# Stick-breaking layer: scores and values as three rounded matmuls instead of one fp32 matmul, with both halves of a later weight split moved behind the gated products

## What is computed

```python
z = jnp.einsum('bqhd,bshd->bhqs', qblk, kk)                      # scores
sp = jnp.where(visible, jax.nn.softplus(z), 0.0)
tw = jnp.einsum('bhqks,sj->bhqkj', sp, upper)                    # sums over later keys
w = jnp.exp(jnp.where(visible, z - tail, -jnp.inf))
return jnp.einsum('bhqs,bshd->bqhd', w, vv)                      # values
...
q, k, v, gate = jnp.split(h @ w_in, [B_WIDTH, 2 * B_WIDTH, 3 * B_WIDTH], axis=-1)
return (o * jax.nn.silu(gate)) @ w_out
```

## Time and profile before

| what | value |
|---|---|
| median of 3 runs (lowest, highest) | 903.99 us (903.72, 904.41) |
| time of the profiled execution | 904.42 us |
| its span, first to last instruction | 902.7 us |
| TensorE busy | 893.0 us, 99% |
| VectorE busy | 551.5 us, 61% |
| ScalarE busy | 430.4 us, 48% |
| chain that ended last | TensorE 96% |

### The profile page before, as it was taken

How to read it: one execution, slowest core, us unless ns; L and a number is a source line. 1 busy time by engine, 2 the same in 40 slices (tenths; PEclk the granted TensorE clock), 3 DMA queues, 4 the chain that set the end, 5 groups by cost and what they waited for, 6 DMA issues and landing times.

```text
span 902.7 us, 17891 instructions
## 1 busy us (share of the span) xinstructions
PE 893.0 (99%) x7182; PEld 861.6 (95%) x7182; DVE 551.5 (61%) x752; ACT 430.4 (48%) x685; POOL 56.4 (6%) x85
## 2 busy tenths in 40 slices
PE   9999999999999999999999999999999999999997
PEld 9999999999999999899999999999999999988886
DVE  6577667666755767785646464555646355545546
ACT  6556455645555344385454443535444444435421
POOL 1322112312200000000000000000000000000000
PEclk9999999999999999999999999999999999999999
DMA  9676465546442555425353434444453534454622
GB/s 351 232 236 180 154 209 134 156 160 190 131 155 114 187 187 191 183 69 211 142 187 139 180 145 169 156 147 178 139 186 139 186 144 165 156 218 156 233 93 94
DMA packets 25256, 153.06 MB, mean 170 GB/s; under 512 B 3410, under 2 KB 3938, under 8 KB 8708
## 3 DMA queue, kind: packets, MB, share of 16 engines
q1 hardware_dynamic: 21600, 142.19, 43.1%
q0 software_dynamic: 2896, 7.70, 4.5%
q10 hardware_dynamic: 724, 2.66, 0.8%
HBM read 150.36 MB, written 2.18 MB: 169 GB/s over the span
## 4 chain that ended last, share of the span: by engine, by line
PE 96%; DMA 1%; DVE 1%; SPq 1%; ACT 0%; issue 0%; DVEq 0%
PE bank L336 72%; PE bank L716 10%; PE bank L495 2%; PE bank L453 2%; DMA work<-chunks 1%; PE bank L661 1%; PE bank L660 1%; PE bank L663 1%; PE bank L628 1%; PE bank L587 1%; PE bank L601 1%; PE bank L470 1%; PE bank L629 0%; PE bank L588 0%; PE bank L471 0%; PE bank L702 0%
## 5 line engine op out<-in xcount | busy, mean ns | idle before, releaser
L336 PE MATMUL bank<-x_hi,w_hi 128*128 128x272 f32 (+1 forms) x1472 | 425.1, 289 | 0.0
L336 PE MATMUL bank<-x_hi,w_lo 128*128 128x272 f32 (+1 forms) x1472 | 421.5, 286 | 0.0
L336 PE MATMUL bank<-x_lo,w_hi 128*128 128x272 f32 (+1 forms) x1472 | 421.4, 286 | 0.0
L1078 DVE TENSOR_TENSOR w_lo<-raw,w_hi 128x2048 fp32r<-128x2048 f32 x126 | 291.0, 2313 | 209.8 <-ACT w_hi L795 177.3
L795 ACT ACTIVATE w_hi<-raw 128x2048 fp32r<-128x2048 f32 x114 | 218.0, 1913 | 156.9 <-PE bank L336 104.5
L336 PEld LDWEIGHTS bank<-x_hi,w_hi 128*128 128x128 f32 x1472 | 277.4, 188 | 0.9 <-issue 0.2
L336 PEld LDWEIGHTS bank<-x_hi,w_lo 128*128 128x128 f32 x1472 | 277.4, 188 | 0.0
L336 PEld LDWEIGHTS bank<-x_lo,w_hi 128*128 128x128 f32 x1472 | 277.1, 188 | 0.0
L336 PE MATMUL bank<-og_hi,w_hi 128*128 128x272 f32 x240 | 70.1, 292 | 0.0
L336 PE MATMUL bank<-og_hi,w_lo 128*128 128x272 f32 x240 | 69.4, 289 | 0.0
L336 PE MATMUL bank<-og_lo,w_hi 128*128 128x272 f32 x240 | 69.1, 288 | 0.0
(11 more groups left out here) (247 smaller groups left out, 1008.4 us busy)
## 6 DMA issues: line engine op xcount, KB each, us to landing
raw<-chunks SPq DMA_DIRECT2D x128, 1024.0 KB, 4.8
work<-bias_table POOLq DMA_DIRECT2D x8, 512.0 KB, 5.7
work<-chunks SPq DMA_DIRECT2D x4, 512.0 KB, 12.6
work<-bias_table POOLq DMA_DIRECT2D x8, 256.0 KB, 6.9
work<-ln_rows ACTq DMA_DIRECT2D x1, 2048.0 KB, 6.9
out<-work SPq DMA_DIRECT2D x8, 256.0 KB, 2.4
h<-xT SPq DMA_DIRECT2D x2, 544.0 KB, 9.2
raw<-chunks SPq DMA_DIRECT2D x4, 256.0 KB, 4.9
```

The source lines that it names most:

```text
L336: last = mm(o, l, r, start=(kt == 0 and n == 0), stop=(kt == KT - 1 and n == 2))
L1078: V.tensor_tensor(lo_part, raw[:, half, :, :], hi_part.bitcast(f32), ALU.subtract) \
```

## The change

Scores and values are made like the projections, from hi and lo parts. For the scores ScalarE makes rounded queries (`qb_parts[0]`) and keys (`kb_parts[0]`) and VectorE the rests; for the values ScalarE makes a rounded copy of the weights w and takes the turned values out of PSUM as rounded, and VectorE makes the rests. The parts lie in buffers that are free at that time (`parts_r`, the last two tiles of `og_hi` and `og_lo`) and two new tiles. Every matmul of `scores_b` and `attend_b` becomes three in fp32r. VectorE's `split_lo(P+5, 0)` and `split_lo(P+5, 1)` both go to the end of the body, behind the gated products. Besides, `neg_ones_r` shrinks to one column that is read 128 times, and a spare identity goes; the spinning matmuls of the layer's start use `neg_upper_r` in its place.

```diff
@@ -89,10 +89,12 @@
...
-        ident_r = sb("ident_r", [128, 128], f32r)
+        last_hi = sb("last_hi", [128, 128], f32r)
+        last_lo = sb("last_lo", [128, 128], f32r)
...
-        neg_ones_r = sb("neg_ones_r", [128, 128], f32r)
+        neg_ones_r = sb("neg_ones_r", [128, 1], f32r)
+        neg_ones = neg_ones_r[:].to_broadcast([128, 128])
@@ -137,8 +139,12 @@
...
-        b = carve([("q", (2, SEQ)), ("kT", (2 * T,)), ("vT", (2 * T,)), ("V", (2, 256)), ("V_last", (128,)),
-                   ("w", (B_Z2,)), ("sp", (B_Z2,)), ("gate", (2, SEQ)), ("og", (SEQ,))])
+        b = carve([("q", (2, SEQ)), ("kT", (2 * T,)), ("vT", (2 * T,)), ("w", (B_Z2,)), ("sp", (B_Z2,)), ("gate", (2, SEQ)), ("og", (SEQ,))])
+        ends = [og.rearrange("p a b -> p (a b)")[:, (KT - 2) * T:KT * T] for og in (og_hi, og_lo)]
+        qb_parts = [flat_r[:, n * 2 * SEQ:(n + 1) * 2 * SEQ].rearrange("p (a b) -> p a b", b=SEQ) for n in range(2)]
+        kb_parts = [flat_r[:, 4 * SEQ:4 * SEQ + 2 * T], ends[1]]
+        vb_parts = [end[:, 0:512].rearrange("p (a b) -> p a b", b=256) for end in ends]
+        vb_last = (last_hi[:], last_lo[:])
@@ -579,17 +587,23 @@
...
             def scores_b(i):

-                for u in range(2):
-                    pe.wait_ge(tile_free[u], P_B + 4 * i + 2)
-                    z, q, k = z_bank[u], b["q"][:, u, :], b["kT"][:, B_KEYS[u]]
-                    if u == 0:
-                        pe.wait_ge(pt_copied, PT_A + 2 * i)
-                    mm(z[:, 0:B_K1], k[:, 0:128], q, start=True, stop=False)
-                    m = mm(z[:, B_K1:B_K2], k[:, 128:256], q[:, B_Q1:SEQ], start=False, stop=(u == 0))
+                pe.wait_ge(qb_lo, i + 1)
+                pe.wait_ge(kb_lo, i + 1)
+                pe.wait_ge(pt_copied, PT_A + 2 * i)
+                terms = [(kb_parts[m], qb_parts[n]) for m, n in ((0, 0), (0, 1), (1, 0))]
+                for u in range(2):
+                    z = z_bank[u]
+                    for n, (k, q) in enumerate(terms):
+                        mm(z[:, 0:B_K1], k[:, B_KEYS[u]][:, 0:128], q[:, u, :], start=(n == 0), stop=False)
+                    for n, (k, q) in enumerate(terms):
+                        m = mm(z[:, B_K1:B_K2], k[:, B_KEYS[u]][:, 128:256], q[:, u, B_Q1:SEQ], start=False,
+                               stop=(u == 0 and n == 2))
                     if u == 0:
                         m.then_inc(z_ready, 1)
                 z = z_bank[1][:, B_K2:B_K2 + B_L]
-                mm(z, b["kT"][:, B_ENDS], b["q"][:, :, B_Q2:SEQ], start=False, stop=True).then_inc(z_ready, 1)
+                for n, (k, q) in enumerate(terms):
+                    m = mm(z, k[:, B_ENDS], q[:, :, B_Q2:SEQ], start=False, stop=(n == 2))
+                m.then_inc(z_ready, 1)
@@ -621,14 +635,20 @@
...
             def attend_b(i):
-                pe.wait_ge(pt_copied, PT_A + 2 * (i + 1))
-                pe.wait_ge(vb_copied, 2 * (i + 1))
-                for u in range(2):
-                    o, w, v = o_b[:, u, :], b["w"][:, B_HEADS[u]], b["V"][:, u, :]
-                    mm(o, v[:, 0:128], w[:, 0:B_K1], start=(u == 0), stop=False)
-                    mm(o[:, B_Q1:SEQ], v[:, 128:256], w[:, B_K1:B_K2], start=False, stop=False)
-                last = b["w"][:, B_LAST].rearrange("p (a c) -> p a c", c=META)
-                mm(o_b[:, :, B_Q2:SEQ], b["V_last"], last, start=False, stop=True).then_inc(pv_done, 2)
+                pe.wait_ge(wb_lo, 2 * (i + 1))
+                pe.wait_ge(vb_lo, 2 * (i + 1))
+                terms = ((0, sp_hi), (1, sp_hi), (0, sp_lo))
+                for u in range(2):
+                    o = o_b[:, u, :]
+                    for n, (m, w) in enumerate(terms):
+                        mm(o, vb_parts[m][:, u, 0:128], w[:, B_HEADS[u]][:, 0:B_K1], start=(u == 0 and n == 0), stop=False)
+                    for m, w in terms:
+                        mm(o[:, B_Q1:SEQ], vb_parts[m][:, u, 128:256], w[:, B_HEADS[u]][:, B_K1:B_K2], start=False,
+                           stop=False)
+                for n, (m, w) in enumerate(terms):
+                    last = mm(o_b[:, :, B_Q2:SEQ], vb_last[m], w[:, B_LAST].rearrange("p (a c) -> p a c", c=META),
+                              start=False, stop=(n == 2))
+                last.then_inc(pv_done, 2)
@@ -990,6 +1009,9 @@
                     split_hi(P + 2, 0, True)
                 for u in range(2):
                     evac(P, u, b["q"][:, u, :], slice(0, SEQ), B_SCALE)
+                for u in range(2):
+                    act.wait_ge(tile_free[u], P + 1)
+                A(qb_parts[0], b["q"], ACT.Copy).then_inc(qb_hi, 1)
                 if not isinstance(i, int):
                     split_hi(P + 2, 1, True)
                     split_hi(P + 3, 0, True)
@@ -999,6 +1021,9 @@
...
                     A(b["kT"][:, B_KEYS[u]] if u else b["kT"][:, 0:T], k_acc[u][:, 0:SEQ if u else T], ACT.Copy) \
                         .then_inc(tile_free[u], 1)
+                for u in range(2):
+                    act.wait_ge(tile_free[u], P + 2)
+                A(kb_parts[0], b["kT"], ACT.Copy).then_inc(kb_hi, 1)
                 if isinstance(i, int):
                     split_hi(P + 3, 0, True)
                 split_hi(P + 3, 1, True)
@@ -1025,10 +1050,12 @@
                 for n, (z, w) in enumerate(parts):
                     act.wait_ge(tail_ready, 2 * i + n + 1)
                     A(w, z, ACT.Exp).then_inc(pt_copied, 1)
+                    act.wait_ge(pt_copied, PT_A + 2 * i + n + 1)
+                    A(sp_hi[:, B_HEADS[n]], w, ACT.Copy).then_inc(wb_hi, 1)
                 act.wait_ge(vtb_ready, 2 * i + 1)
-                A(b["V"].rearrange("p a b -> p (a b)"), v_turned[:], ACT.Copy).then_inc(vb_copied, 1)
+                A(vb_parts[0].rearrange("p a b -> p (a b)"), v_turned[:], ACT.Copy).then_inc(vb_copied, 1)
                 act.wait_ge(vtb_ready, 2 * i + 2)
-                A(b["V_last"], bank[5][:, 0:128], ACT.Copy).then_inc(vb_copied, 1)
+                A(vb_last[0], bank[5][:, 0:128], ACT.Copy).then_inc(vb_copied, 1)
@@ -1357,9 +1384,18 @@
             def body_b(i):
                 P = P_B + 4 * i

+                def queries_rest():
+                    dve.wait_ge(qb_hi, i + 1)
+                    V.tensor_tensor(qb_parts[1], b["q"], qb_parts[0].bitcast(f32), ALU.subtract).then_inc(qb_lo, 1)
+
                 if not isinstance(i, int):
+                    queries_rest()
                     split_lo(P + 2, 0, True)
                 split_lo(P + 2, 1, True)
+                if isinstance(i, int):
+                    queries_rest()
+                dve.wait_ge(kb_hi, i + 1)
+                V.tensor_tensor(kb_parts[1], b["kT"], kb_parts[0].bitcast(f32), ALU.subtract).then_inc(kb_lo, 1)
                 split_lo(P + 3, 0, True)
                 split_lo(P + 3, 1, True)
@@ -1390,7 +1426,15 @@
                     if u == 0 and isinstance(i, int):
                         split_lo(P + 4, 0, True)
                 split_lo(P + 4, 1, True)
-                split_lo(P + 5, 0, True)
+                for n, (z, w, s) in enumerate(parts):
+                    dve.wait_ge(wb_hi, 2 * i + n + 1)
+                    V.tensor_tensor(sp_lo[:, B_HEADS[n]], w, sp_hi[:, B_HEADS[n]].bitcast(f32), ALU.subtract) \
+                     .then_inc(wb_lo, 1)
+                dve.wait_ge(vb_copied, 2 * i + 1)
+                V.tensor_tensor(vb_parts[1].rearrange("p a b -> p (a b)"), v_turned[:],
+                                vb_parts[0].rearrange("p a b -> p (a b)").bitcast(f32), ALU.subtract).then_inc(vb_lo, 1)
+                dve.wait_ge(vb_copied, 2 * i + 2)
+                V.tensor_tensor(vb_last[1], bank[5][:, 0:128], vb_last[0].bitcast(f32), ALU.subtract).then_inc(vb_lo, 1)
                 for u in range(2):
@@ -1400,7 +1444,6 @@
...
                     V.tensor_tensor(b["gate"][:, u, :], acc[u][:, 0:SEQ], b["gate"][:, u, :], ALU.mult) \
                      .then_inc(tile_free[u], 1)
-                split_lo(P + 5, 1, True)
                 for u in range(2):
                     dve.wait_ge(pv_done, PV_A + 2 * i + u + 1)
                     dve.wait_ge(tile_free[u], P + 4)
@@ -1410,6 +1453,8 @@
...
                     V.tensor_tensor(og_lo[:, 2 * i + u, 0:SEQ], b["og"], og_hi[:, 2 * i + u, 0:SEQ].bitcast(f32),
                                     ALU.subtract).then_inc(og_lo_ready, 1)
+                split_lo(P + 5, 0, True)
+                split_lo(P + 5, 1, True)
```

More of the change, by code:

```diff
@@ L213, in trunk @@
         tail_ready, vtb_ready, vb_copied = sem("tail_ready"), sem("vtb_ready"), sem("vb_copied")
+        qb_hi, qb_lo, kb_hi, kb_lo = sem("qb_hi"), sem("qb_lo"), sem("kb_hi"), sem("kb_lo")
+        wb_hi, wb_lo, vb_lo = sem("wb_hi"), sem("wb_lo"), sem("vb_lo")
         gateb_exp, gateb_den, rs_guess = sem("gateb_exp"), sem("gateb_den"), sem("rs_guess")
@@ L552, in spin @@
                 for _ in range(count):
```

(13 more changed lines are left out.)

## The result

The changed kernel takes 965.51 us (median of 4 runs, 963.94 to 966.43) against 903.86: a ratio of 1.068 (95% interval 1.067 to 1.069), 62 us slower. The forecast was 947.5, with 930 to 962 as its range: the direction and both waits were right, and the time lies 3.5 us above the range.

What follows compares the result with a forecast made beforehand. TensorE, busy 99%, was taken to set the time. 904.4 us plus 42.7 for loop waits (7 x (3.1 + 2.8 + 0.2)), plus 2 for the first iteration, minus 1 for matmuls gave 948, as median 947.5; range 930 to 962.

Steps and rivals of the forecast that it cites:

- two hand-overs: Queries' copies 2.5 us ahead of the keys' projection; values' copy ending 0.5 us before the gates' projection starts.
- the first wait: Before the keys' projection, TensorE waits 3.1 us for ScalarE's queries' copy, behind a late-loaded values split; 7 loop iterations.
- the second: Before the gates' projection, TensorE waits 2.8 us for VectorE's values' copy, after a late next-queries load and split; 7 times.
- the first iteration: Differently ordered splits and two added roundings ahead of ScalarE's splits cost 2 us, bounds 0 and 3.
- the clock falls: Rival, 10%: fourteen 3 us waits each bring an equally long stretch at 1.2 GHz, costing 21 us; 968 us in all.
- the likeliest case: Both loop waits at full clock: 947.5 us, own range 936 to 956, given 65%.
- TensorE's own work: Scores and values blocks with three fp32r matmuls per fp32 one: -1 us over 16 blocks, bounds -6 and +2.
- the tails' rows: Profile rows of 144- and 32-column fp32r matmuls, 0.087 and 0.093 us each, giving a scores block of 1.50 us against 1.50.
- friendlier neighbours: Scores and values blocks: 0.06 us taken off each of 16, since the rows are of weight loads repeating one matrix.

Runs made afterwards that it cites:

- the waits filled: Changed kernel plus 22 unused 256-column matmuls ahead of the keys' and of the gates' projection in each loop iteration: 946.34 us, ratio 1.047.
- the matmuls alone: Kernel before with only the scores' and values' fp32 matmuls replaced by three fp32r each, on other data, attention not computed: 905.93 us, ratio 1.0024.
- both orders mended: Changed kernel with both P+5 splits back in place, keys' rest behind the gates' first split, queries' rest behind the values' first split: 908.55 us, ratio 1.0049.
- the splits back: Changed kernel with both VectorE splits of pair P+5 put back where the kernel before had them: 929.74 us, ratio 1.028.
- the keys' rest later: Changed kernel with the VectorE rest of the keys moved behind the gates' first split instead of ahead of it: 934.08 us, ratio 1.034.
- the queries' copies ahead: Changed kernel with the queries' copies on ScalarE moved ahead of the late split of the values' first chunk: 933.44 us, ratio 1.032.

## Why the prediction was wrong

**What bounds the kernel, and the mechanism: right.** The reading that TensorE has no slack, that two hand-overs are narrow, and that the order of VectorE turns into late loads held in every run. (The room at the queries' copies is 2.2 us and not the 2.5 that the prediction's first paragraph gives: the first copy ends at 600.47 and the keys' projection begins at 602.7. Its sum doesn't use the 2.5.) TensorE's list has the first wait, forecast at 3.1 us, at 2.6 to 3.0 (19.5 / 7 = 2.8), and the second, forecast at 2.8, at 2.35 (16.9 less the first iteration's 0.47, over 7). The list counts from the modelled end of the last matmul, 0.28 us after its start, where the next one would have started after 0.12; so the stream stands still 0.16 us longer than listed, 2.9 and 2.5 us. The first matmul after a wait takes 0.20 us to the next start instead of 0.13 (571.85 to 572.05): 0.07 more, where the forecast had 0.1. Together that is 39 us in the loop against the forecast's 42.7. The half-rate stretches don't explain why the second wait is shorter: with the waits filled and the clock full, the values' copy ends 2.4 us after the fill began (591.65 to 594.01), as long as in the changed kernel.

**The step that failed: the clock.** The prediction held "the clock falls" as a rival at 10%, priced it well (half of 3 us, 14 times, 21 us, and 968 in all), and put the likeliest case and the whole range on the side where a wait of 3 us does nothing to the rate. The granted clock fell at 13 of 14 waits, and filling the waits gave 19.2 us back. With the clock at full rate the same kernel takes 946.3, fill included, against a forecast of 947.5. That these agree to 1 us is partly luck: the forecast had the waits 3.5 us and the first iteration 1 us too dear, and TensorE's own work 3 us too cheap. So the error is one decision: "no row shows that a wait of this length does it" is no evidence that it doesn't. The rows of before could not tell, since they had no wait over 1.1 us, and an untried case belonged in the range at something like even chances. The rule cited there, of a half-rate default that idleness brings back (the Trainium skill, "TensorE: Matmul & The Clock Gate", part 1), agrees with this trace in that half rate goes with idleness: 0.50 from 572.4 to 575.7, behind a wait of 2.6 us, and none where the waits were filled.

**TensorE's own work: mis-sized, with the wrong sign.** Forecast -1 us, measured +2.2 (the matmuls alone). The working from the tails' rows gave 0; the 0.06 us a block that I then took off for "friendlier neighbours" had no row behind it. In the changed kernel the scores take 1.63 us against 1.50: three matmuls of 144 columns take 0.29 us (591.95 to 592.24), so 0.10 each and not 0.087 as between two with the same matrix, and the three of 256 columns of the second head take 0.40 instead of 0.35. That the change of weights costs the difference is likely, and no run tries it apart. Three for one never showed as a gain at 144 and 32 columns; at 256 it did, 0.08 us of 0.44.

**First iteration: too dear.** Forecast +2 us, with bounds of 0 and 3. In the changed kernel TensorE has one wait there that the kernel before hasn't, for the values' copy:

```profile
422.50 0.39 PE L344 MATMUL bank<-x_hi,w_hi 128*128 128x256 f32 x1 [0.47 <-DVE work L1424]
```

By the estimate above that costs 0.7 us. From the start of its first scores to that of the next 58.16 us pass, 5.7 more than before; the first of the loop's long waits (3.0, so 3.2 us), its half-rate stretch (1.5) and the two dearer blocks (0.3) are 5.0 of them, which leaves about the same 0.7. Ahead of its first scores nothing is lost. With both orders mended more is left, 4.6 less 2.2 for the matmuls, 2.4 us, but that kernel has waits in the first iteration that the changed one hasn't.

**The sum.** 36.4 us of waits in TensorE's list, 3.4 for what the list leaves out at 15 waits (0.16 and 0.07 each), 19.2 for the clock and 2.2 for the matmuls make 61.2 of the 61.7 us between the medians. The first iteration's wait is in the list. The terms were measured in separate kernels, so half a us is as close as this sum can come.

**Open.** Not every wait brings a half-rate stretch, and its length doesn't decide it. In the changed kernel 13 of 14 do, with the splits back four of seven (waits of 2.3 us), with the keys' rest later four of seven, in the kernel before with the moved splits five of seven; in the last two a wait of 3.0 us brought none, while two and three of the stretches are 6.8 us long. With the queries' copies ahead, three waits of 1.8 to 2.0 us brought one each. The mean clock differs between executions of one kernel too (0.976 to 0.985 in the kernel with the moved splits alone). What decides it was not tried.

## What to carry to other kernels

Where a load waits for an operation on an in-order engine, everything ahead of that operation is ahead of the load. A 0.7 us subtraction that waits for the end of a projection, put in front of such a split, cost 31 us; behind it, 0.7 us once. So before moving anything on a "non-critical" engine, follow what its completion triggers, and then what stands behind that trigger's consumer on the next engine.

Price a wait of TensorE that the trace has no like of at its length and at its length and a half, and keep both in the range; and read the mean clock and the distance between starts, since slices and busy time hide a half-rate stretch.

Three fp32r matmuls for one fp32 matmul paid here at 256 columns only: keep short fp32 matmuls as they are.

## What the hardware showed that was not expected

- Waits of 2.2 to 3.0 us brought TensorE to 1.2 GHz in 13 of 14 cases, and waits of 1.8 to 2.0 us in 3 of 7 (the second waits of the kernel with the queries' copies ahead). The half rate mostly falls on useful work: in the iteration shown the wait ends at 571.85, TensorE runs at full rate at first, and the half rate shows from 572.4 to 575.7. Matmuls whose results are thrown away, in the wait, prevent it: 965.5 to 946.3 us.
- An fp32r matmul of 32 columns costs about 0.1 us between starts (0.30 us for three, 592.93 to 593.23 in the changed kernel), hardly less than one of 256 columns, 0.118. An fp32 one of 32 columns costs 0.14.
